# Neighbourhood attention: K/Q projections of the next head group placed between the tiles of this one, with two K and Q buffers

## The reference, cut to what matters

```
u = h @ w_in                       # h: (2048, 1024) normalised tokens, hc: (256, 1024) context
q, k, v = u[q cols], u[k cols], u[v cols]      # 8 heads of 64
ck, cv  = (hc @ w_in)[k, v cols]
s_win = q . k (8 x 16 window) * 64**-0.5 + rpb # -1e30 outside the window
s_ctx = q . ck * 64**-0.5
p = softmax(concat(s_win, s_ctx))
y_d = p_win @ v + p_ctx @ cv
y = concat(y_c, y_d) * silu(z)     # z: gate columns of u; y_c: Fourier branch
x = x + gate * (y @ w_out)
```

## Time and profile before

| | |
|---|---|
| median of 3 runs | 1902.68 us (1902.41 to 1951.13) |
| profiled execution, slowest core | 1897.03 us |
| its span, first to last instruction | 1895.4 us |
| spans of the eight cores | 1873.3 to 1895.4 us |
| busy: TensorE, VectorE, ScalarE, GpSimd | 61%, 46%, 41%, 12% |
| granted TensorE clock, mean of that core | 0.831 of full |
| ACT_TABLE_LOAD in the program | 22 |

### The profile page before, as it was taken

The page is one execution under the profiler, slowest core; times in us unless marked ns, Lnnn a source line. Parts: engine busy times, 40 slices in busy tenths (PEclk is TensorE's granted clock), DMA queues, the critical chain, the costliest instruction groups (busy, mean ns, idle before and its releaser), DMA issues.

```text
span 1895.4 us, 20058 instructions; the slowest of 8 cores (1873.3 to 1895.4 us)
## 1 busy us (share of the span) xinstructions
PE 1156.7 (61%) x6289; PEld 545.7 (29%) x6289; DVE 880.5 (46%) x1243; ACT 773.6 (41%) x1089; POOL 230.5 (12%) x169
## 2 busy tenths in 40 slices
PE   0445556333332778787876776254986877777383
PEld 0232223111111223222322332142433343444131
DVE  0360799864445445455545446062022242343276
ACT  0371122123333668686876300083111265566221
POOL 1014766010000100000000000010000100000001
PEclk9757788666666899999998888655999899989798
DMA  7534000020000100000000167945110422200445
GB/s 107 126 121 67 1 1 1 0 59 1 0 1 1 23 1 1 1 1 1 1 1 1 36 187 238 150 144 124 67 67 1 62 29 34 26 10 1 89 142 180
DMA packets 53079, 99.38 MB, mean 52 GB/s; under 512 B 15733, under 2 KB 34513, under 8 KB 51824
## 3 DMA queue, kind: packets, MB, share of 16 engines
q0 software_dynamic: 35712, 32.18, 11.6%
q1 hardware_dynamic: 17264, 65.92, 10.9%
HBM read 112.44 MB, written 17.83 MB: 69 GB/s over the span
## 4 chain that ended last, share of the span: by engine, by line
PE 39%; DVE 20%; DMA 12%; ACT 11%; issue 10%; POOL 7%; DVEq 1%; ACTq 0%; SPq 0%; POOLq 0%
PE PS L123 38%; ACT ARENA L129 9%; DVE ARENA L132 8%; POOL ARENA L132 4%; DVE ARENA L153 4%; DMA W<-w_ada 4%; DVE ARENA L141 2%; POOL ARENA L147 2%; DMA W<-w_in 2%; DMA W<-w_out 2%; DMA XT<-x 2%; DVE HT L138 1%; DVE YT L132 1%; ACT ARENA L145 1%; PE PS L126 1%
## 5 line engine op out<-in xcount | busy, mean ns | idle before, releaser
L123 PE MATMUL PS<-ARENA 128*128 128x512 bf16 (+4 forms) x3100 | 513.5, 314 | 178.0 <-ACT ARENA L129 80.2
L129 ACT ACTIVATE ARENA<-PS 128x1024 bf16<-128x1024 f32 (+5 forms) x580 | 480.1, 865 | 248.0 <-PE PS L123 235.6
L123 PEld LDWEIGHTS PS<-ARENA 128*128 128x128 bf16 x3100 | 223.7, 99 | 454.6 <-issue 324.0
L123 PE MATMUL PS<-HT,W 128*128 128x512 bf16 (+3 forms) x1216 | 267.3, 379 | 40.1 <-DMA W<-w_in 21.4
L141 DVE SCALAR_TENSOR_TENSOR ARENA<-ARENA,CW 128x2319 f32<-128x2319 f32 x64 | 186.6, 2916 | 66.0 <-ACT ARENA L129 59.4
L153 DVE RECIPROCAL ARENA<-ARENA 64x512 f32<-64x512 f32 (+3 forms) x45 | 136.2, 3028 | 128.7 <-ACT ARENA L145 116.1
L145 ACT ACTIVATE ARENA<-PS 128x512 f32<-128x512 f32 (+6 forms) x156 | 82.0, 539 | 248.8 <-PE PS L123 193.9
L132 DVE TENSOR_TENSOR ARENA<-ARENA 128x256 f32<-128x256 f32 (+5 forms) x244 | 132.9, 560 | 97.7 <-ACT ARENA L129 79.4
L123 PEld LDWEIGHTS PS<-HT,W 128*128 128x128 bf16 x1216 | 120.2, 102 | 183.3 <-issue 79.6
L123 PE MATMUL PS<-W,YT 128*128 128x512 bf16 x544 | 126.3, 388 | 62.7 <-DMA W<-w_out 41.9
L123 PE MATMUL PS<-W,HT 128*128 128x512 bf16 (+1 forms) x560 | 113.7, 362 | 28.2 <-DMA W<-w_in 28.2
(11 more groups left out here) (67 smaller groups left out, 763.1 us busy)
## 6 DMA issues: line engine op xcount, KB each, us to landing
XT<-xs SPq DMA_DIRECT2D x29, 512.0 KB, 3.6
XT<-x SPq DMA_DIRECT2D x27, 512.0 KB, 4.1
W<-w_ada POOLq DMA_DIRECT2D x12, 1024.0 KB, 10.9
xs<-ARENA SPq DMA_DIRECT2D x18, 512.0 KB, 3.5
ARENA<-dft SPq DMA_DIRECT2D x8, 1024.0 KB, 5.3
out<-ARENA SPq DMA_DIRECT2D x16, 512.0 KB, 3.0
W<-w_in POOLq DMA_DIRECT2D x5, 1024.0 KB, 15.1
W<-w_out POOLq DMA_DIRECT2D x2, 2048.0 KB, 18.6
```

Source lines behind the costliest of these rows:

```text
L123: self.op('pe', lambda e: e.matmul(out, lhsT, rhs, start=start, stop=stop), r, w)
L129: self.op('act', lambda e: e.activation(out, in_, func, **kw), r, w)
```

## The change

- There are two K buffers and two Q buffers, and group `hg` uses number `hg % 2`. The second Q buffer is filled with zeros by GpSimd as the first is.
- The projection of a group is cut into nine steps: five K steps (eight matmuls and one VectorE copy) and four Q steps (eight matmuls and two VectorE `tensor_scalar` of 64 partitions each). All use bank 7. VectorE evacuates where ScalarE did.
- Group 0's nine steps run before the loops. Those of group `hg + 1` stand in the loop of group `hg`, one behind P.V of each of the tiles 2 to 10.
- The Q and K weights and the bias table of group `hg + 1` are loaded at the head of group `hg`.
- The gate projections of all four groups stand behind the last loop, with one weight load of 512 columns into W1, issued at the head of group 3, and two `SZ` buffers.

```diff
--- before.py
+++ after.py
@@ -901,7 +901,7 @@
         SZ = AR.alloc([512], F32)
         wload(W0, 'W0', w_in_d[1], 1536, 512, 0)
         p.ms('dve', VA, 1.0, w=['VA'])
-        p.ms('pool', QAB, 0.0, w=['QAB'])
+        p.ms('pool', QAB, 0.0, w=['QAB0'])
         for t in range(NT):
             bi = 6 + t % 2
             for k in range(KC):
@@ -910,39 +910,70 @@
             p.cp('act' if t % 2 == 0 else 'dve', VA[:, t, :, 0:64], bank(bi).rearrange("p (h d) -> p h d", h=8),
                  r=[PB[bi]], w=['VA'])
         EBGs = [EBG, AR.alloc([2, NP, 128], BF16)]
-        for hg in range(4):
-            Wn, wnk = (W1, 'W1') if hg % 2 == 0 else (W0, 'W0')
-            EBG, ebk = EBGs[hg % 2], f'EBG{hg % 2}'
+        KT2s = [KT2, AR.alloc([T], BF16)]
+        QABs = [QAB, AR.alloc([NTL, 2, 128], BF16)]
+        p.ms('pool', QABs[1], 0.0, w=['QAB1'])
+
+        def Wof(hg):
+            return (W1, 'W1') if hg % 2 == 0 else (W0, 'W0')
+
+        def loadpair(hg):
+            Wn, wnk = Wof(hg)
             wload(Wn, wnk, w_in_d[1], 512 + hg * 128, 128, 0)
             wload(Wn, wnk, w_in_d[1], 1024 + hg * 128, 128, 128)
-            wload(Wn, wnk, w_in_d[1], 2048 + 512 + hg * 128, 128, 256)
+            EBG, ebk = EBGs[hg % 2], f'EBG{hg % 2}'
             p.dma('pool', EBG, bm_d[:, hg, :].rearrange("p (h a q) -> p h a q", h=2, q=128), writes=[ebk], sem=ebk)
+
+        def projsteps(hg):
+            Wn, wnk = Wof(hg)
+            kt2, ktk = KT2s[hg % 2], f'KT2{hg % 2}'
+            qab, qk_ = QABs[hg % 2], f'QAB{hg % 2}'
+            steps = []
+            for (b0, bn) in BLOCKS:
+                def kstep(b0=b0, bn=bn):
+                    hk = ht_keys(b0, bn)
+                    for k in range(KC):
+                        p.mm(bank(7)[:, 0:bn], Wn[:, k, 128:256], HT[:, k, b0:b0 + bn],
+                             start=(k == 0), stop=(k == KC - 1), r=[wnk] + hk, w=[PB[7]])
+                    p.cp('dve', kt2[:, b0:b0 + bn], bank(7)[:, 0:bn], r=[PB[7]], w=[ktk])
+                steps.append(kstep)
+            for (b0, bn) in BLOCKS[:4]:
+                def qstep(b0=b0, bn=bn):
+                    hk = ht_keys(b0, bn)
+                    for k in range(KC):
+                        p.mm(bank(7), Wn[:, k, 0:128], HT[:, k, b0:b0 + bn],
+                             start=(k == 0), stop=(k == KC - 1), r=[wnk] + hk, w=[PB[7]])
+                    src3 = bank(7).rearrange("p (t n) -> p t n", t=4)
+                    p.ts('dve', qab[0:64, b0 // 128:b0 // 128 + 4, 0, :], src3[0:64], 0.125, None, ALU.mult, None,
+                         r=[PB[7]], w=[qk_])
+                    p.ts('dve', qab[64:128, b0 // 128:b0 // 128 + 4, 1, :], src3[64:128], 0.125, None, ALU.mult, None,
+                         r=[PB[7]], w=[qk_])
+                steps.append(qstep)
+            return steps
+
+        def Jof(i):
+            return na_tiles[i] + [(16, None), (17, None)]
+
+        loadpair(0)
+        for st_ in projsteps(0):
+            st_()
+        for hg in range(4):
+            EBG, ebk = EBGs[hg % 2], f'EBG{hg % 2}'
+            kt2, ktk = KT2s[hg % 2], f'KT2{hg % 2}'
+            qab, qk_ = QABs[hg % 2], f'QAB{hg % 2}'
             p.act(EBG, EBG, AF.Exp, r=[ebk], w=[ebk])
-            for bi_, (b0, bn) in enumerate(BLOCKS):
-                hk = ht_keys(b0, bn)
-                bi = 6 + bi_ % 2
-                for k in range(KC):
-                    p.mm(bank(bi)[:, 0:bn], Wn[:, k, 128:256], HT[:, k, b0:b0 + bn],
-                         start=(k == 0), stop=(k == KC - 1), r=[wnk] + hk, w=[PB[bi]])
-                p.cp('act', KT2[:, b0:b0 + bn], bank(bi)[:, 0:bn], r=[PB[bi]], w=['KT2'])
-            for bi_, (b0, bn) in enumerate(BLOCKS[:4]):
-                hk = ht_keys(b0, bn)
-                bi = 6 + bi_ % 2
-                for k in range(KC):
-                    p.mm(bank(bi), Wn[:, k, 0:128], HT[:, k, b0:b0 + bn],
-                         start=(k == 0), stop=(k == KC - 1), r=[wnk] + hk, w=[PB[bi]])
-                src3 = bank(bi).rearrange("p (t n) -> p t n", t=4)
-                p.act(QAB[0:64, b0 // 128:b0 // 128 + 4, 0, :], src3[0:64], AF.Copy, r=[PB[bi]], w=['QAB'], scale=0.125)
-                p.act(QAB[64:128, b0 // 128:b0 // 128 + 4, 1, :], src3[64:128], AF.Copy, r=[PB[bi]], w=['QAB'], scale=0.125)
-
-            def Jof(i):
-                return na_tiles[i] + [(16, None), (17, None)]
+            nxt = []
+            if hg + 1 < 4:
+                loadpair(hg + 1)
+                nxt = projsteps(hg + 1)
+            else:
+                wload(W1, 'W1', w_in_d[1], 2048 + 512, 512, 0)
 
             def qkg(i):
                 for idx, (j, pat) in enumerate(Jof(i)):
                     bi = idx // 2
-                    p.mm(bank(bi)[:, (idx % 2) * 256:(idx % 2 + 1) * 256], KT2[:, j * 128:(j + 1) * 128],
-                         QAB[:, i, :, :], r=['KT2', 'QAB'], w=[PB[bi]])
+                    p.mm(bank(bi)[:, (idx % 2) * 256:(idx % 2 + 1) * 256], kt2[:, j * 128:(j + 1) * 128],
+                         qab[:, i, :, :], r=[ktk, qk_], w=[PB[bi]])
 
             EBv = EBG.rearrange("p h a q -> p a h q")
 
@@ -984,18 +1015,26 @@
                     for idx, (j, pat) in enumerate(J):
                         p.mm(bank(pob)[:, h * 65:(h + 1) * 65], pt[:, idx, h, :], VA[:, j, 2 * hg + h, :],
                              start=(idx == 0), stop=(idx == nj - 1), r=[ptk + 'a', ptk + 'b', 'VA'], w=[PB[pob]])
+                if 2 <= i < 2 + len(nxt):
+                    nxt[i - 2]()
             postA(NTL - 1)
             postC(NTL - 1)
+        n_ = 0
+        SZ2 = [SZ, AR.alloc([512], F32)]
+        for j in range(4):
             for kb in range(4):
                 b0 = kb * 512
                 hk = ht_keys(b0, 512)
-                bi = 6 + kb % 2
+                bi = 6 + n_ % 2
+                sz = SZ2[n_ % 2]
+                szk = f'SZ{n_ % 2}'
+                n_ += 1
                 for k in range(KC):
-                    p.mm(bank(bi), Wn[:, k, 256:384], HT[:, k, b0:b0 + 512],
-                         start=(k == 0), stop=(k == KC - 1), r=[wnk] + hk, w=[PB[bi]])
-                p.act(SZ, bank(bi), AF.Silu, r=[PB[bi]], w=['SZ'])
-                p.tt('dve', YT[:, 4 + hg, b0:b0 + 512], YT[:, 4 + hg, b0:b0 + 512], SZ, ALU.mult,
-                     r=[f'YT{4 + hg}', 'SZ'], w=[f'YT{4 + hg}'])
+                    p.mm(bank(bi), W1[:, k, j * 128:(j + 1) * 128], HT[:, k, b0:b0 + 512],
+                         start=(k == 0), stop=(k == KC - 1), r=['W1'] + hk, w=[PB[bi]])
+                p.act(sz, bank(bi), AF.Silu, r=[PB[bi]], w=[szk])
+                p.tt('dve', YT[:, 4 + j, b0:b0 + 512], YT[:, 4 + j, b0:b0 + 512], sz, ALU.mult,
+                     r=[f'YT{4 + j}', szk], w=[f'YT{4 + j}'])
 
     phases = [lambda: adaln(0), lambda: phase_norm(0), phase_conv, phase_attn, lambda: phase_out(0),
               lambda: adaln(1), lambda: phase_norm(1), phase_fourier, phase_na, lambda: phase_out(1)]
```

## The result

The changed kernel takes 1931.4 us (median of 10 runs) where the kernel before takes 1902.5 (10 runs on the same chip). The ratio is 1.0151 with a 95% interval of 1.0132 to 1.0169: 1.5% slower, 29 us. Medians are over all runs; ratios leave out the runs in which a die ran at a lower clock. The direction and the range of the forecast held; the size was twice what I had worked out, +29 for +14.

A forecast was written before the change was run, and what follows sets the result against it. Waits between engines, in the loop a VectorE-TensorE-VectorE ring, were taken to bound the kernel. -85.9 + 20.8 + 9.2 + 71.1 - 1.2 = +14.0 us gave 1917 us, 0.75% slower, range 1899 to 1936.

The forecast's parts named there:

- What is removed: Three stretches between the loops, with gate and next K/Q projections, go as a whole, bias exponentials covered: -85.9 us.
- Gates at the end: Final gate stretch after the last loop grows by 12 blocks of 1.73 us, from 10.54 to 31.3 us: +20.8 us.
- The first projection: Group 0's nine steps before the loops, all in bank 7 with VectorE evacuating: 26.5 against 17.37 us, +9.2 us.
- The steps inside the loops: Tiles 2 to 10 of loops 0 to 2 each lengthen by a whole K or Q step: +71.1 us.
- the joins: Between loops, the next group's first scores follow the transpose, not the copy behind it: some 0.4 us less each, -1.2 us.
- The splice: In step tiles, matmuls and evacuation come between P·V and RECIPROCAL in the VectorE-TensorE ring; tiles become 4.6 or 5.4 us.
- The forecast mechanism: Whole steps lengthen the loop tiles at full clock; 1900 to 1930 us, own bounds 1908 and 1921, chance 0.78.
- rival 2: TensorE's clock falls to half in step tiles, each step costing 1.73 us more: 1964 us; chance 0.09, also in part.
- Rival 1: Steps fill TensorE's idle time inside the loops, tiles of 3.2 us: 1872 us; chance 0.13, also in part.
- Rival 3: Q evacuations cost 0.42 us each (1908) or 0.12 more (1921) instead of 0.69; within the forecast's range, no separate chance.

The follow-up runs named there:

- the filler experiment: Against the changed kernel, eight unread 256-column matmuls added behind the scores in tiles 7 to 11 of loops 0 to 2: 1918.1 us, ratio 1.0109 to the kernel before.
- the deferred kernel: Against the changed kernel, each step's evacuation moved on VectorE from ahead of the next RECIPROCAL to behind the next bias multiply: 1870.7 us, ratio 0.9856 to the kernel before.

## Why the prediction was right in direction, and half the size

- **What is removed** (-85.9): right. The stretches are gone, and no wait on a weight transfer stands in their place. In the profile after, the bias exponentials of groups 1 to 3 are covered (the one at 1608.56 lasts 2.77 us and ends at 1611.3, 1.5 us before the first exponential of scores).
- **Gates at the end** (+20.8): 31.45 against 10.54 is +20.9. By the Trainium skill, "ScalarE: Activation LUTs", section "What ACT_TABLE_LOAD costs", it would be 1.4 us more. The trace doesn't agree: the load at 1784.14 takes 1.28 us and the first Silu starts at 1785.43. The profile counts 16 table loads instead of 22, as forecast.
- **The first projection** (+9.2): +11.1. A K step takes 2.83 us and not 2.63. I took 1.73 for a block from blocks that follow each other, 0.07 for its release; a block that stands alone takes 1.89 in the timeline and is released 0.1 later. Nine times 0.2 is the difference, about.
- **The steps inside the loops** (+71.1 with -1.2 at the joins): this term was mis-sized. The four loops together take 234.1 us against 222.1. The splice itself was right to 3%: K tile 4.46 (forecast 4.6), Q tile at full clock 5.37 (forecast 5.4), the RECIPROCAL without a wait, Q evacuations of 0.689 us. Deferring the evacuation, which takes the splice away and nothing else, took 53 us off, the clock's share among them. What the sum put at nothing was the clock: on average 6.75 of a core's 24 long blocks run at 1.2 GHz, each making its tile 7.0 us instead of 5.4. Seven times 1.67 is 11.7 us, and the filler experiment took 12.4 off. The forecast mechanism's own bounds, 1908 and 1921, don't hold the 1931.4. The range did, by its upper end, which I had drawn where a dozen slow steps would lie; that it was wide enough is owed to rival 2 and not to the sum.
- **Rival 2** therefore came true in part. I held against it that the new tiles are as dense as the old ones. They nearly are: 3.55 of 5.37 us busy is 66%, against 69% in the earlier trace rows, and yet the clock fell. A Q tile differs from a K tile (74% busy) and from one with fillers (77%) by its busy share, and by the wait of 1.57 us that it leaves, instead of 0.65 or 0.70. Neither alone is a rule. In the four Q steps of the first projection, in this same trace, TensorE is busy 51% of the time with waits of 1.74 us, and the granted clock stays at 1.00 in them on all eight cores. On three cores it falls 1.0 to 1.1 us behind their end. Core 4, a window over the four steps and a block in it:

```profile
1532.26:1546.77 14.51, 7.33 (x32) 2.85 (x34) 5.51 (x8) 0.00 (x0) 0.89 (x1) 1.00 0.00 0
...
1543.14 1.89 PE L123 MATMUL PS<-HT,W 128*128 128x512 bf16 x8 [1.74 <-DVE ARENA L136]
```

The trace agrees in part with the Trainium skill, "TensorE: Matmul & The Clock Gate", section "A second HAM failure mode: psum-queue depth-cycling", on small idles between groups, which I had set aside. Read as it stands, though, it would have the clock swing in the K tiles and in the first projection too, and there it stays at 1.00. Why the clock falls behind some Q steps of the loops and not behind others, and not within the first projection, stays open; the runs show that it differs between cores and loops.
- **Rival 1**, with steps in TensorE's idle time, was wrong for this kernel, but its tile comes near to that of the kernel with the deferred evacuation: 3.2 us were worked out, 2.97 (K) and 3.63 (Q) measured. That its 1872 us almost meets the 1870.7 measured is in part luck. Rival 1 had 31 us less than the kernel before; the stage of the deferred kernel is 24.8 us shorter, and the kernel before ran some 5 us faster beside it.
- **Rival 3** (evacuations of 0.42 or 0.81 us): 0.689. The middle was right.

The three missed terms add up: 1.9 from the first projection, 12.0 from the loops, 0.1 from the gates make 14.0, and with the forecast 14.0 the 28.0 us by which the stage grew between the two traces.

## What to carry to other kernels

When work is put into another loop, follow it in every queue that it enters, not only in the one whose idle time it is to fill: an evacuation ahead of the next link of a dependency ring adds the producer's whole time to the ring, and in this kernel it cost 53 us less a few lines further down in the same queue. Where a tile gets longer by waits, price TensorE's work in it at both clock levels and put that into the sum with a weight: here neither the busy share nor the length of a wait told beforehand which tiles would fall. When an engine joins in a job, look for what stood behind on its queue under the cover of its idleness.

## What the runs showed of the hardware that I had not expected

- With TensorE busy 66% of each tile, in pieces, the granted clock fell to 0.50 in some tiles, behind a wait of 1.57 us; with fillers in the same tiles (77% busy, wait 0.70) it stayed at 1.00. In the four Q steps of the first projection, busy 51% with waits of 1.74, it stayed at 1.00 too.
- 120 useless matmuls of 256 columns on each core made the stage 12.4 us shorter.
- A block of eight 512-column matmuls with nothing behind it takes 1.89 us in the trace; in a row a block comes every 1.73 us.
